# Layer 1's FFN output: sums of weights made by accumulating transfers, and eight pairs in place of seven

## The chip, the core and the metric

One core of a Trainium2 chip runs the whole kernel. The metric is the device time in microseconds, the median of several runs. Engines are called TensorE (PE in the rows, PEld its weight loads), VectorE (DVE), ScalarE (ACT), GpSimd (POOL) and SyncE (SP, which here only issues transfers). A name with a q behind it (SPq) is an engine's instruction queue.

## The reference

Two layers of a streaming encoder on x of 256 tokens by 2048, in float32. The change lies in the last product of the second layer's FFN:

```python
h = rmsnorm(x, norm_ffn[l])
gu = h @ w_ffn_in[l]                                   # 2048 x (2 * 5504)
g = causal_dwconv(gu[..., :D_FF], ffn_conv_w[l], ffn_conv_b[l])
x = x + (jax.nn.silu(g) * gu[..., D_FF:]) @ w_ffn_out[l]   # (256 x 5504) @ (5504 x 2048)
...
return rmsnorm(x, final_norm)
```

Layers are counted from 0: layer 1 is the last.

## The kernel before

**Weights as a stream.** All large weights come from HBM in pieces of 128 partitions by 1024 columns of float32 (512 KB), in the order of their use, into a ring of four buffers `raw`. For each piece ScalarE writes a rounded copy to `whi` (the high half), VectorE writes the rest, `raw - whi`, to `wlo` (the low half), and TensorE takes both. `whi` and `wlo` are rings of four slots too. A float32 product is three matmuls: high by high, high by low and low by high. Each engine walks the pieces in one fixed order, written out by hand; hooks (`at(idx, fn)`) put other work behind a given slot.

**The FFN output.** `hidden` holds the 43 chunks of 128 rows of the hidden layer, as the stationary operand by high and low half. The 2048 output columns are done in two halves u = 0, 1 of 1024, each of which has two strips f of 512 columns (`COLS`) and two blocks t of 128 tokens. A chunk by itself (a "single") has one piece and one slot: four block products, 12 matmuls of 512 columns.

**Pairs by seven products.** Two chunks k1, k2 with two strips and two blocks of tokens are a 2 by 2 block product, which the kernel computes by seven block products in place of eight (Strassen's way, in Winograd's form). This unit takes two pieces, own = (a, b) and second = (d, c), and four slots: "own" (6 matmuls), "fe" (6), "gh" (6) and "d" (3). VectorE makes four sums of the weights: e and f together as one wide addition into the buffer `fe` (line 1188), then g and h into `gh` (lines 1192 and 1194). Their buffers lie in the memory of `gt` and `half`, so the rows show them by these names: `gt<-raw` is the sum fe, `half<-raw,gt` and `half<-raw,half` are g and h, and `wlo<-gt,whi` is the low half of fe. The sums of the hidden layer's blocks ("combinations") are made by VectorE in batches of two pairs (`combs_add`, lines 1203 to 1222, and `combs_low`, 1224), each four or five additions and then a low half, and stay for both halves u.

**The order of units** is given by `units_of`. Both layers have seven pairs, (8, 9), (13, 14) and so on: in half 0 eight singles, then pair, three singles, pair, and so on; in half 1 four singles come first. After the seventh pair half 0 has three and half 1 seven singles. `COMBS_AT` says behind which slot each batch is added; its low half follows one slot later, behind everything that VectorE does for that slot.

**Waits.** ScalarE's high half of slot n waits for TensorE to free slot n - 4 (`slot_released`), VectorE's low half for the high half, TensorE for the low half. SP loads the next piece into a ring buffer when its last reader is through (`wait_read`): for the first piece of a pair this is the sum h, for its second the low half of d. After the last pair of a half the seven products are read out of PSUM: `products_upper` behind the slot five after fe, `products_lower` behind the next; in layer 1 they write to the memory of `gt` and `half` too. TensorE takes the last three slots (`LAST_TAIL`) together: per strip and block, each of the three singles in turn. Then the last strips are added, normalised and stored.

**GpSimd** does a few additions for the mixer of each layer, and nothing in the FFN.

Of the kernel before, what the change touches and what calls it, by code (L numbers as in the profile page):

```python
# [23 lines left out]
LAYERS = 2  # L24
DM = 2048
S = 256
P = 128
# [10 lines left out]
RING = 4  # L38
PB = 8
PIECE = PB * P  # L40
# [17 lines left out]
D0 = CT + 12  # L58
# [9 lines left out]
LO0 = 1  # L68
# [25 lines left out]
COLS = NT * P  # L94
# [13 lines left out]
    return ends  # L108

PAIRED = tuple([(8 + 5 * i, 9 + 5 * i) for i in range(7)] for _ in range(LAYERS))
LEADS = ((8, 4), (8, 4))
PARTS = ("own", "fe", "gh", "d")

def units_of(l, u):

    single = [k for k in range(FC) if not any(k in pair for pair in PAIRED[l])]
    lead, rest = single[:LEADS[l][u]], single[LEADS[l][u]:]
    units = [(k,) for k in lead]  # L120
    for i, pair in enumerate(PAIRED[l]):
        units += [pair] + [(k,) for k in rest[3 * i:3 * i + 3]]
    return units + [(k,) for k in rest[3 * len(PAIRED[l]):]]

def slots_of(l):
# [10 lines left out]
def wraps(piece):  # L137
    return piece % RING == RING - 1

OUT_SLOTS = tuple(slots_of(l) for l in range(LAYERS))
# [5 lines left out]
Q_BANKS = ((4, 5, 6, 7), (0, 1, 2, 3))  # L147
LAST_TAIL = 3
TURN_AT = (1, 1, 3, 3, 5, 5, 6, 6)
COMBS_AT = ((5, 12, 26, 40), (5, 12, 26, 40))  # L150

ENDS = dict(group_ends())
# [24 lines left out]
def program(nc, xT, wstream, params, lamv, consts, poolw, pww, gain_rows, outT):  # L178
# [5 lines left out]
    ALU, ACT, AX = mybir.AluOpType, mybir.ActivationFunctionType, mybir.AxisListType  # L184

    ctx = ExitStack()
    with ctx:
# [8 lines left out]
        def sem(name):  # L196
            return ctx.enter_context(nc.semaphore(name))
# [16 lines left out]
        rest = sb("rest", [P, DM])  # L214
# [6 lines left out]
        raw = sb("raw", [P, RING, PIECE])  # L221
# [135 lines left out]
        front_scaled = [sem(f"front_scaled{t}") for t in range(2)]  # L357
        back_scaled = [sem(f"back_scaled{t}") for t in range(2)]
        sum_ready = sem("sum_ready")
        combs_added, combs_hi, combs_ready = sem("combs_added"), sem("combs_hi"), sem("combs_ready")  # L360
        m1_copied = sem("m1_copied")
        products_read = sem("products_read")
# [28 lines left out]
        def landed(piece):  # L391
            return (piece // RING + 1) * 16
# [13 lines left out]
        def strip(l, u, f, t):  # L406
            c = (2 * u + f) * COLS
            return xt[:, t, c:c + COLS] if l else outs[:, f, t, :]

        block = ctx.enter_context(nc.Block())  # L410

        @block.sync
        def _(sp):
            sp.dma_start(raw[:, 0, 0:PIECE // 2], wstream[0, :, 0:PIECE // 2]).then_inc(half_landed, 16)
            sp.dma_start(raw[:, 0, PIECE // 2:], wstream[0, :, PIECE // 2:]).then_inc(raw_landed[0], 16)

            def load_x(part):
                c, n = X_PARTS[part]
                sp.dma_start(x[:, c:c + n, :], xT[:, c:c + n, :]).then_inc(x_loaded[part], 16)  # L420

            for s in range(1, RING):
                if s > 1:
                    load_x(s)
                sp.dma_start(raw[:, s, :], wstream[s, :, :]).then_inc(raw_landed[s], 16)
            for part in (4, 5):
                load_x(part)

            def load_next(r, s, old):
                sp.wait_ge(lo_ready, old + 1 + LO0)  # L430
                sp.dma_start(raw[:, s, :], wstream[bass.ds(r * RING + s, 1), :, :]
                             .rearrange("o p c -> p (o c)")).then_inc(raw_landed[s], 16)

            def wait_read(l, idx):

                if idx < D0:
                    sp.wait_ge(lo_ready, W0[l] + idx + 1 + LO0)
                    return
                table = OUT_SLOTS[l]
                n = max(m for m, o in enumerate(table) if o[3] <= idx - D0)  # L440
                if table[n][1] != "one" and table[n][3] == idx - D0:
                    sp.wait_ge(sum_ready, SUMS0[l] + 3 * sum(1 for o in table[:n + 1] if o[1] == "d"))
# [30 lines left out]
        def _(act):  # L473
# [28 lines left out]
            for l in range(LAYERS):  # L502
# [179 lines left out]
                def out_hi(n):  # L682

                    u, part, unit, piece = OUT_SLOTS[l][n]
                    s, q = (W0[l] + D0 + n) % RING, sum(1 for o in OUT_SLOTS[l][:n] if o[1] == "d")
                    piece += R0[l] + D0
                    wide = COLS if part == "d" else PIECE
                    if part in ("one", "own"):
                        act.wait_ge(raw_landed[piece % RING], landed(piece))
                        src = raw[:, piece % RING, :]  # L690
                    elif part == "d":
                        act.wait_ge(raw_landed[(piece + 1) % RING], landed(piece + 1))
                        src = raw[:, (piece + 1) % RING, 0:COLS]
                    elif part == "fe":
                        act.wait_ge(sum_ready, SUMS0[l] + 3 * q + 1)
                        src = fe
                    else:
                        act.wait_ge(sum_ready, SUMS0[l] + 3 * q + 3)
# [201 lines left out]
        def _(dve):  # L900
# [30 lines left out]
            for l in range(LAYERS):  # L931
# [236 lines left out]
                def out_lo(n):  # L1168
# [10 lines left out]
                    src = {"one": raw[:, first, :], "own": raw[:, first, :], "fe": fe, "gh": gh, "d": d}[part]  # L1179
                    nc.vector.tensor_tensor(wlo[:, s, 0:wide], src, whi[:, s, 0:wide], ALU.subtract).then_inc(lo_ready, 1)  # L1180
                    if part == "own":
                        dve.wait_ge(raw_landed[second], landed(piece + 1))
                        if q:
                            dve.wait_ge(lo_ready, base + max(m for m in range(n) if OUT_SLOTS[l][m][1] == "gh") + 1 + LO0)
                        if u:
                            dve.wait_ge(products_read, 2 * l + u)
                        a_and_d = raw[:, 0:RING:RING - 1, 0:COLS] if wraps(piece) else raw[:, first:second + 1, 0:COLS]
                        nc.vector.tensor_tensor(fe.rearrange("p (h c) -> p h c", h=2), a_and_d,  # L1188
                                                c[:, None, :].to_broadcast([P, 2, COLS]), ALU.add).then_inc(sum_ready, 1)
                        dve.wait_ge(sum_ready, SUMS0[l] + 3 * q + 1)  # L1190
                        e = fe[:, 0:COLS] if wraps(piece) else fe[:, COLS:PIECE]
                        nc.vector.tensor_tensor(gh[:, 0:COLS], a, e, ALU.add).then_inc(sum_ready, 1)
                        dve.wait_ge(sum_ready, SUMS0[l] + 3 * q + 2)
# [9 lines left out]
                def combs_add(b):  # L1203
# [8 lines left out]
                    pairs = hidden[:, k:k + 5 * n, :].rearrange("p (i j) c -> p i j c", j=5)[:, :, 0:2, :]  # L1212
# [269 lines left out]
        def _(pool):  # L1482
# [6 lines left out]
            for l in range(LAYERS):  # L1489
# [21 lines left out]
                nc.gpsimd.tensor_tensor(win1[:, 1, 15:W], win0[:, 1, 15:W], win0[:, 1, 7:W - 8],  # L1511
                                        ALU.add).then_inc(windowed, 1)
                SEEN["pool"] = st.n

        @block.tensor
        def _(pe):
# [4 lines left out]
            for l in range(LAYERS):  # L1522
# [307 lines left out]
                def seven(n):  # L1830
# [25 lines left out]
                            last.then_inc(acc_done, 1)  # L1856
                        three(C_BANKS[u][0][0], *tokens(k2, 0), *weights(n, 1), False, False).then_inc(slot_free, 1)
                    elif part == "fe":
                        f_at = 1 if wraps(piece) else 0
# [123 lines left out]
```

## Time and profile before

| | us |
|---|---|
| median of 3 runs (2060.15 to 2060.85) | 2060.2 |
| the profiled execution | 2060.9 |
| its span, first to last instruction | 2059.1 |
| busy: TensorE / VectorE / ScalarE / GpSimd | 2046.9 / 1565.3 / 1129.9 / 23.5 |
| layer 1's FFN output, first to last matmul start | 1821.16 to 2051.21 |

The rows are of one profiled execution. Times of a timeline count from the span's start. Busy times of TensorE overlap, since its matmuls are pipelined: the step from one start to the next is what a matmul costs. "Idle before" is the time in which the engine stood still ahead of an instruction, with what ended it behind the arrow.

### The profile page before, as it was taken

Reading aid. Unit: us, or ns where it says so; the run is one execution under the profiler, and the core shown is the slowest. Engines: PE = TensorE matmul, PEld = TensorE weight load, DVE = VectorE, ACT = ScalarE, POOL = GpSimd, SP = SyncE. Lnnn points to the kernel's source line nnn. Section 1 sums busy time; section 2 is a strip of 40 time slices with the busy share of each in tenths; the row PEclk is TensorE's granted clock in tenths of the full one; section 3 lists DMA queues with packets and bytes.
Section 4 is the critical chain, followed back from the end, with each engine's and each line's share of the span. In section 5 each row is a group of like instructions: output and inputs, shape, how many; then the busy total and the mean of one; then the engine's idle time right before and its main releaser. Section 6 shows DMA issues by size and latency. Waiting matters only on the chain.

```text
span 2059.1 us, 31630 instructions
## 1 busy us (share of the span) xinstructions
PE 2046.9 (99%) x11168; PEld 1764.5 (86%) x11168; DVE 1565.3 (76%) x2198; ACT 1129.9 (55%) x1573; POOL 23.5 (1%) x20
## 2 busy tenths in 40 slices
PE   9999999999999999999999999999999999999998
PEld 8888888888888888788888888888888888887887
DVE  7998777676666677988789978677666767679887
ACT  6555655555555555555564556455455555555554
POOL 0001100000000000000000011000000000000000
PEclk9999999999999999999999999999999999999999
DMA  8554355655555655566565544655555565555664
GB/s 292 176 184 164 134 186 182 203 187 194 191 185 182 203 185 183 195 203 199 200 212 196 176 154 144 190 191 191 194 189 188 181 199 190 194 164 194 199 224 170
DMA packets 107942, 389.59 MB, mean 189 GB/s; under 512 B 12112, under 2 KB 12624, under 8 KB 107472
## 3 DMA queue, kind: packets, MB, share of 16 engines
q1 hardware_dynamic: 105984, 383.30, 56.3%
q10 hardware_dynamic: 1872, 5.13, 0.7%
q8 instruction: 56, 0.92, 0.2%
q14 instruction: 30, 0.25, 0.0%
HBM read 386.28 MB, written 2.10 MB: 189 GB/s over the span
## 4 chain that ended last, share of the span: by engine, by line
PE 96%; DVE 3%; ACT 0%; DMA 0%; issue 0%; DVEq 0%; ACTq 0%
PE bank L1524 46%; PE bank L1527 23%; PE bank L1794 6%; PE bank L1796 6%; PE bank L1795 6%; PE bank L1621 2%; PE bank L1600 1%; PE bank L1602 1%; PE bank L1601 1%; DVE wlo L1180 1%; DMA x<-xT 0%; ACT whi L701 0%; PE bank L1674 0%; DVE combs L1227 0%; DVE gt L1188 0%
## 5 line engine op out<-in xcount | busy, mean ns | idle before, releaser
L1524 PE MATMUL bank<-xg,whi 128*128 128x512 f32 x3648 | 1135.8, 393 | 2.1 <-DVE wlo L919 2.1
L938 DVE TENSOR_TENSOR wlo<-raw,whi 128x1024 fp32r<-128x1024 f32 x556 | 676.7, 1223 | 374.2 <-ACT whi L520 373.5
L520 ACT ACTIVATE whi<-raw 128x1024 fp32r<-128x1024 f32 x556 | 582.8, 1057 | 438.8 <-PE bank L1527 419.2
L1527 PEld LDWEIGHTS bank<-xg,wlo 128*128 128x128 f32 x3648 | 685.0, 188 | 151.1
L1527 PE MATMUL bank<-xg,wlo 128*128 128x256 f32 x3648 | 720.0, 279 | 0.0
L1524 PEld LDWEIGHTS bank<-xg,whi 128*128 128x128 f32 x3648 | 552.9, 188 | 6.7 <-issue 3.3
L1180 DVE TENSOR_TENSOR wlo<-raw,whi 128x1024 fp32r<-128x1024 f32 (+1 forms) x164 | 183.1, 1132 | 55.4 <-ACT whi L701 50.6
L1794 PE MATMUL bank<-whi,hidden 128*128 128x512 f32 x548 | 214.4, 391 | 0.9 <-DVE wlo L1180 0.9
L1796 PE MATMUL bank<-whi,hidden 128*128 128x512 f32 x548 | 213.3, 389 | 0.0
L1795 PE MATMUL bank<-wlo,hidden 128*128 128x512 f32 x548 | 213.2, 389 | 0.0
L701 ACT ACTIVATE whi<-raw 128x1024 fp32r<-128x1024 f32 (+1 forms) x164 | 159.4, 984 | 93.3 <-PE bank L1796 82.3
L1524 PE MATMUL bank<-mix,whi 128*128 128x512 f32 x512 | 160.7, 395 | 0.0
L1794 PEld LDWEIGHTS bank<-whi,hidden 128*128 128x128 f32 x548 | 102.9, 188 | 24.0 <-DVE wlo L1180 2.6
L1796 PEld LDWEIGHTS bank<-whi,hidden 128*128 128x128 f32 x548 | 102.9, 188 | 21.5
L1795 PEld LDWEIGHTS bank<-wlo,hidden 128*128 128x128 f32 x548 | 102.9, 188 | 21.0
L525 ACT ACTIVATE half<-bank 128x256 f32<-128x256 f32 x228 | 86.1, 382 | 62.6 <-PE bank L1527 60.1
L1527 PEld LDWEIGHTS bank<-mix,wlo 128*128 128x128 f32 x512 | 96.1, 188 | 21.2
L996 DVE SCALAR_TENSOR_TENSOR gt<-glu,par,gt 128x256 f32<-128x256 f32 x240 | 101.4, 487 | 0.0
L1527 PE MATMUL bank<-mix,wlo 128*128 128x256 f32 x512 | 101.1, 279 | 0.0
L1524 PEld LDWEIGHTS bank<-mix,whi 128*128 128x128 f32 x512 | 78.3, 188 | 0.8
L701 ACT ACTIVATE whi<-gt 128x1024 fp32r<-128x1024 f32 x28 | 29.8, 1063 | 77.3 <-DVE gt L1188 77.3
L1305 DVE SCALAR_TENSOR_TENSOR y<-gt,par,y 128x256 f32<-128x256 f32 x172 | 70.0, 480 | 0.0
(212 smaller groups left out, 1499.2 us busy)
## 6 DMA issues: line engine op xcount, KB each, us to landing
raw<-wstream SPq DMA_DIRECT2D x723, 512.0 KB, 3.4
pw_sb<-pww ACTq DMA_DIRECT2D x2, 1024.0 KB, 7.5
outT<-xt SPq DMA_DIRECT2D x6, 256.0 KB, 2.2
x<-xT SPq DMA_DIRECT2D x2, 512.0 KB, 10.4
gains<-gain_rows ACTq DMA_DIRECT2D x1, 1024.0 KB, 6.0
raw<-wstream SPq DMA_DIRECT2D x2, 256.0 KB, 4.0
x<-xT ACTq DMA_DIRECT2D x2, 256.0 KB, 5.4
x<-xT SPq DMA_DIRECT2D x2, 256.0 KB, 7.6
```

The source lines that it names most:

```text
L520: nc.scalar.activation(whi[:, s, slot_cols(rel)], raw[:, source, :], ACT.Copy).then_inc(hi_ready, 1)
L525: nc.scalar.activation(half[:, i, :], ps[b][:, S:2 * S], ACT.Copy, scale=scales[i]).then_inc(half_ready, 1)
L701: nc.scalar.activation(whi[:, s, 0:wide], src, ACT.Copy).then_inc(hi_ready, 1)
L938: nc.vector.tensor_tensor(wlo[:, s, slot_cols(rel)], raw[:, source, :], whi[:, s, slot_cols(rel)], ALU.subtract).then_inc(lo_ready, 1)
L996: ins = nc.vector.scalar_tensor_tensor(out=gt[:, i, 0:S], in0=glu[:, i, k:k + S], scalar=w, in1=gt[:, i, 0:S], op0=ALU.mult, op1=ALU.add)
L1180: nc.vector.tensor_tensor(wlo[:, s, 0:wide], src, whi[:, s, 0:wide], ALU.subtract).then_inc(lo_ready, 1)
L1305: ins = nc.vector.scalar_tensor_tensor(out=y[:, i, :], in0=gt[:, i, k:k + S], scalar=par[:, bass.ds(col, 1)], in1=y[:, i, :], op0=ALU.mult ...
L1524: nc.tensor.matmul(ps[bank][:], whi[:, s, blk * P:blk * P + P], mov, start=first, stop=False)
L1527: return nc.tensor.matmul(ps[bank][:, 0:S], wlo[:, s, blk * P:blk * P + P], mov[:, 0:S], start=False, stop=last)
L1794: nc.tensor.matmul(ps[bank][:], xh, wh, start=first, stop=False)
L1795: nc.tensor.matmul(ps[bank][:], xh, wl, start=False, stop=False)
L1796: return nc.tensor.matmul(ps[bank][:], xl, wh, start=False, stop=last)
```

## The change

In layer 1 alone, pairs become (8, 9), (12, 13), ... (36, 37): eight of them, at a stride of four. `BETWEEN` gives the singles between two pairs: in half 0 five times two, then two times three; in half 1 four times three, then three times two. After the last pair half 0 has three singles and half 1 has five. The batches of combinations move to slots 5, 13, 25 and 37, and the fourth is full.

In layer 1 the sum fe leaves VectorE. SP loads (a, d) from HBM straight into `fe`, 512 KB in rows of 2 KB, and GpSimd then issues two transfers that add c (256 KB each, from HBM) to its two halves. SP issues the load of the next unit behind the weight load that replaces own, and waits there for the low half of fe; the first waits for the hidden layer to be done, the first of half 1 for the readout of half 0's products. VectorE's g and h, and ScalarE's high half of fe, wait for the second accumulate. VectorE's sums no longer wait for the second piece.

```diff
-PAIRED = tuple([(8 + 5 * i, 9 + 5 * i) for i in range(7)] for _ in range(LAYERS))
+STRIDE = (5, 4)
+PAIRED = tuple([(8 + STRIDE[l] * i, 9 + STRIDE[l] * i) for i in range(n)] for l, n in enumerate((7, 8)))
+BETWEEN = (((3,) * 6, (3,) * 6), ((2, 2, 2, 2, 2, 3, 3), (3, 3, 3, 3, 2, 2, 2)))
+SUMMED = (3, 2)
...
-COMBS_AT = ((5, 12, 26, 40), (5, 12, 26, 40))
+COMBS_AT = ((5, 12, 26, 40), (5, 13, 25, 37))
...
+            owns = own_pieces(1)
+            half_units = len(PAIRED[1])
+            load_fe_behind = {D0 + 4: 0, D0 + owns[half_units - 1] + 6: half_units}
+            for q in range(len(owns) - 1):
+                if q + 1 != half_units:
+                    load_fe_behind[D0 + owns[q]] = q + 1
+
+            def load_fe(q):
+                if q == 0:
+                    sp.wait_ge(hidden_ready, FFG + FFG)
+                elif q == half_units:
+                    sp.wait_ge(products_read, 3)
+                else:
+                    sp.wait_ge(lo_ready, W0[1] + D0 + fe_slots(1)[q - 1] + 1 + LO0)
+                piece = R0[1] + D0 + owns[q]
+                sp.dma_start(fe_halves, wstream[piece:piece + 2, :, 0:COLS].rearrange("o p c -> p o c")).then_inc(fe_landed, 16)
...
                     sp.dma_start(raw[:, piece % RING, :], wstream[piece, :, :]).then_inc(raw_landed[piece % RING], 16)
+                    if l and old - R0[1] in load_fe_behind:
+                        load_fe(load_fe_behind[old - R0[1]])
...
                     elif part == "fe":
-                        act.wait_ge(sum_ready, SUMS0[l] + 3 * q + 1)
+                        if l:
+                            act.wait_ge(fe_summed, 32 * q + 32)
+                        else:
+                            act.wait_ge(sum_ready, SUMS0[l] + SUMMED[l] * q + 1)
...
-                        dve.wait_ge(raw_landed[second], landed(piece + 1))
+                        if l == 0:
+                            dve.wait_ge(raw_landed[second], landed(piece + 1))
...
-                        a_and_d = raw[:, 0:RING:RING - 1, 0:COLS] if wraps(piece) else raw[:, first:second + 1, 0:COLS]
-                        nc.vector.tensor_tensor(fe.rearrange("p (h c) -> p h c", h=2), a_and_d,
-                                                c[:, None, :].to_broadcast([P, 2, COLS]), ALU.add).then_inc(sum_ready, 1)
+                        if l:
+                            dve.wait_ge(fe_summed, 32 * q + 32)
+                            e = fe[:, COLS:PIECE]
...
+            for q, own in enumerate(own_pieces(1)):
+                pool.wait_ge(fe_landed, 16 * q + 16)
+                second = R0[1] + D0 + own + 1
+                for h in range(2):
+                    pool.dma_start(fe_halves[:, h, :], wstream[second, :, COLS:PIECE], accum_op=ALU.add).then_inc(fe_summed, 16)
```

## Rows read from the trace of the kernel before

**Rows 1.** The page: busy time, share of the span, instructions.

```profile
PE 2046.9 (99%) x11168; PEld 1764.5 (86%) x11168; DVE 1565.3 (76%) x2198; ACT 1129.9 (55%) x1573; POOL 23.5 (1%) x20
```

**Rows 2.** Timeline of TensorE in the stage: start, us, engine, line, operation.

```profile
1821.16 0.39 PE L1794 MATMUL bank<-whi,hidden 128*128 128x512 f32 x1
1821.39 0.40 PE L1795 MATMUL bank<-wlo,hidden 128*128 128x512 f32 x1
...
1826.62 1.03 PE L1790 MATMUL bank<-con,x 128*128 128x128 f32 x8
...
2051.21 0.39 PE L1796 MATMUL bank<-whi,hidden 128*128 128x512 f32 x1
```

**Rows 3.** Groups of TensorE from 1821 to 2052 us, first of three lines.

```profile
L1794 PE MATMUL bank<-whi,hidden 128*128 128x512 f32 x274 | 107.3, 392 | 0.5 <-DVE wlo L1180 0.4
...
L1794 PE MATMUL bank<-whi,combs 128*128 128x512 f32 x56 | 22.0, 393 | 0.2
```

**Rows 4.** Waits of TensorE's weight loads, 1820 to 2052: total, times, longest.

```profile
PEld bank L1794 <- DVE wlo L1180: 2.3, 4, 0.6
PEld bank L1794 <- DVE xt L1264: 0.5, 1, 0.5
```

**Rows 5.** Stretches: length, busy PE, PEld, DVE, ACT, POOL, clock, DMA share, GB/s.

```profile
1850.00:1875.00 25.00, 24.69 (x108) 19.79 (x107) 23.69 (x26) 13.15 (x15) 0.00 (x0) 1.00 0.60 204
...
1950.00:1975.00 25.00, 25.00 (x112) 20.72 (x111) 20.14 (x20) 15.68 (x22) 0.00 (x0) 1.00 0.62 207
```

**Rows 6.** Timeline of VectorE around a batch and the sums of the second unit.

```profile
1849.29 1.23 DVE L1180 TENSOR_TENSOR wlo<-raw,whi 128x1024 fp32r<-128x1024 f32 x1 [1.10 <-ACT whi L701]
1850.43 1.22 DVE L1214 TENSOR_TENSOR rest<-hidden 128x1024 f32<-128x1024 f32 x1
...
1853.16 1.22 DVE L1180 TENSOR_TENSOR wlo<-raw,whi 128x1024 fp32r<-128x1024 f32 x1
...
1857.78 1.22 DVE L1188 TENSOR_TENSOR gt<-raw 128x1024 f32<-128x1024 f32 x1
...
1860.37 1.22 DVE L1180 TENSOR_TENSOR wlo<-gt,whi 128x1024 fp32r<-128x1024 f32 x1
```

**Rows 7.** Timeline of TensorE around that batch, and at the last pair.

```profile
1847.93 0.39 PE L1794 MATMUL bank<-whi,combs 128*128 128x512 f32 x1
...
1853.83 0.39 PE L1796 MATMUL bank<-whi,hidden 128*128 128x512 f32 x1
1854.43 0.50 PE L1794 MATMUL bank<-whi,hidden 128*128 128x512 f32 x1 [0.22 <-DVE wlo L1180]
...
1861.16 0.39 PE L1796 MATMUL bank<-whi,hidden 128*128 128x512 f32 x1
1861.64 0.50 PE L1794 MATMUL bank<-whi,combs 128*128 128x512 f32 x1
...
2028.99 0.39 PE L1794 MATMUL bank<-whi,combs 128*128 128x512 f32 x1
```

**Rows 8.** Timeline of VectorE behind the last pair.

```profile
2034.21 0.68 DVE L1241 TENSOR_TENSOR xt<-bank,xt 128x512 f32<-128x512 f32 x1
...
2040.65 3.49 DVE L1180 TENSOR_TENSOR wlo<-raw,whi 128x1024 fp32r<-128x1024 f32 x3
```

**Rows 9.** One weight load issued 1871.7 to 1873, one 1864.4 to 1865.6: KB, us to landing.

```profile
raw<-wstream SPq DMA_DIRECT2D x1, 512.0 KB, 3.2
...
raw<-wstream SPq DMA_DIRECT2D x1, 512.0 KB, 4.4
```

**Rows 10.** Transfers of 256 KB of the whole kernel: count, KB, median us to landing.

```profile
outT<-xt SPq DMA_DIRECT2D x6, 256.0 KB, 2.2
...
poolw_sb<-poolw ACTq DMA_DIRECT2D x2, 256.0 KB, 6.4
```

**Rows 11.** Timeline of GpSimd, layer 1's mixer: two additions of one shape.

```profile
1201.32 2.21 POOL L1494 TENSOR_TENSOR sq<-gt 128x512 f32<-128x512 f32 x1 [962.62 <-DVE gt L996]
...
1217.59 1.29 POOL L1499 TENSOR_TENSOR sq<-y 128x512 f32<-128x512 f32 x1 [12.36 <-ACT y L593]
```

More of the change, by code:

```diff
@@ L121, in units_of @@
     for i, pair in enumerate(PAIRED[l]):
-        units += [pair] + [(k,) for k in rest[3 * i:3 * i + 3]]
-    return units + [(k,) for k in rest[3 * len(PAIRED[l]):]]
+        begin = sum(BETWEEN[l][u][:i])
+        units += [pair] + [(k,) for k in (rest[begin:begin + BETWEEN[l][u][i]] if pair != PAIRED[l][-1] else rest[begin:])]
+    return units
 def slots_of(l):
@@ L359, in program @@
         sum_ready = sem("sum_ready")
+        fe_landed, fe_summed = sem("fe_landed"), sem("fe_summed")
         combs_added, combs_hi, combs_ready = sem("combs_added"), sem("combs_hi"), sem("combs_ready")
@@ L408, in strip, with own_pieces, fe_slots @@
             return xt[:, t, c:c + COLS] if l else outs[:, f, t, :]
+        fe_halves = fe.rearrange("p (h c) -> p h c", h=2)
+        def own_pieces(l):
+            return [o[3] for o in OUT_SLOTS[l] if o[1] == "own"]
+        def fe_slots(l):
+            return [n for n, o in enumerate(OUT_SLOTS[l]) if o[1] == "fe"]
         block = ctx.enter_context(nc.Block())
@@ L441, in wait_read @@
                 if table[n][1] != "one" and table[n][3] == idx - D0:
-                    sp.wait_ge(sum_ready, SUMS0[l] + 3 * sum(1 for o in table[:n + 1] if o[1] == "d"))
+                    sp.wait_ge(sum_ready, SUMS0[l] + SUMMED[l] * sum(1 for o in table[:n + 1] if o[1] == "d"))
                 else:
                     sp.wait_ge(lo_ready, W0[l] + D0 + n + 1 + LO0)
+            owns = own_pieces(1)
[13 more added lines that the diff above has]
+                sp.dma_start(fe_halves, wstream[piece:piece + 2, :, 0:COLS].rearrange("o p c -> p o c")).then_inc(fe_landed, 16)
             def load_each(first, end):
@@ L694, in out_hi @@
                     elif part == "fe":
-                        act.wait_ge(sum_ready, SUMS0[l] + 3 * q + 1)
+                        if l:
+                            act.wait_ge(fe_summed, 32 * q + 32)
+                        else:
+                            act.wait_ge(sum_ready, SUMS0[l] + SUMMED[l] * q + 1)
                         src = fe
                     else:
-                        act.wait_ge(sum_ready, SUMS0[l] + 3 * q + 3)
+                        act.wait_ge(sum_ready, SUMS0[l] + SUMMED[l] * (q + 1))
                         src = gh
@@ L1186, in out_lo @@
                             dve.wait_ge(products_read, 2 * l + u)
-                        a_and_d = raw[:, 0:RING:RING - 1, 0:COLS] if wraps(piece) else raw[:, first:second + 1, 0:COLS]
-                        nc.vector.tensor_tensor(fe.rearrange("p (h c) -> p h c", h=2), a_and_d,
-                                                c[:, None, :].to_broadcast([P, 2, COLS]), ALU.add).then_inc(sum_ready, 1)
-                        dve.wait_ge(sum_ready, SUMS0[l] + 3 * q + 1)
-                        e = fe[:, 0:COLS] if wraps(piece) else fe[:, COLS:PIECE]
+                        if l:
+                            dve.wait_ge(fe_summed, 32 * q + 32)
+                            e = fe[:, COLS:PIECE]
+                        else:
+                            a_and_d = raw[:, 0:RING:RING - 1, 0:COLS] if wraps(piece) else raw[:, first:second + 1, 0:COLS]
+                            nc.vector.tensor_tensor(fe_halves, a_and_d, c[:, None, :].to_broadcast([P, 2, COLS]),
+                                                    ALU.add).then_inc(sum_ready, 1)
+                            dve.wait_ge(sum_ready, SUMS0[l] + SUMMED[l] * q + 1)
+                            e = fe[:, 0:COLS] if wraps(piece) else fe[:, COLS:PIECE]
                         nc.vector.tensor_tensor(gh[:, 0:COLS], a, e, ALU.add).then_inc(sum_ready, 1)
-                        dve.wait_ge(sum_ready, SUMS0[l] + 3 * q + 2)
+                        dve.wait_ge(sum_ready, SUMS0[l] + SUMMED[l] * (q + 1) - 1)
                         nc.vector.tensor_tensor(gh[:, COLS:PIECE], b, gh[:, 0:COLS], ALU.add).then_inc(sum_ready, 1)
@@ L1211, in combs_add @@
                     n = len(PAIRED[l][2 * b:2 * b + 2])
-                    pairs = hidden[:, k:k + 5 * n, :].rearrange("p (i j) c -> p i j c", j=5)[:, :, 0:2, :]
+                    pairs = hidden[:, k:k + STRIDE[l] * n, :].rearrange("p (i j) c -> p i j c", j=STRIDE[l])[:, :, 0:2, :]
                     r = tokens_raw[l][b].rearrange("p (i j c) -> p i j c", i=2, j=2)[:, 0:n]
@@ L1858, in seven @@
                     elif part == "fe":
-                        f_at = 1 if wraps(piece) else 0
+                        f_at = 1 if wraps(piece) and l == 0 else 0
                         last = three(Q_BANKS[u][M5], *comb(0), *weights(n, f_at), first, final)
```

## The prediction

> **What bounds the kernel now.** I read four views in this order: the page's busy times, the waits of TensorE inside the stage that the change touches, the order of VectorE's work just before two of those waits, and the stage by stretches. [rows 1] TensorE is busy for 99% of the span and VectorE for 76%: the end moves only with the number of matmuls or with moments in which TensorE finds no weights. The stage is layer 1's FFN output, from 1821.16 us to the last matmul start at 2051.21 us [rows 2], with (274 + 56) x 3 = 990 matmuls of 512 columns [rows 3]. The mean duration there, 0.39 us, is not the price of one, since they overlap: starts go by in steps of 0.227 us (1821.16, 1821.39; 0.23 as printed) [rows 2]. 990 x 0.2267 = 224.4 us; the four groups of eight transposes take about 1.0 us each [rows 2]; so of the stage's 230.3 us some 1.9 us are stalls. They are few: TensorE's weight loads wait four times for a low half, 2.3 us with what would be idle anyway, and once for a readout [rows 4]. The granted clock is 1.00, the upper of the two levels, throughout [rows 5].
>
> VectorE is close behind. Its busy time is 23.69 of 25 us in a stretch that holds a batch of combinations, 20.14 of 25 us in one without [rows 5]. So the order of VectorE's work decides whether TensorE waits, and less its sum. Its own durations: a full low half 1.22 us, started every 1.14 us; the sum fe 1.22 (1.26 to the next start); the two sums g and h 1.34 together (the low half of fe starts 2.59 us after the sum fe); a batch's additions 2.73 (1850.43 to 1853.16) [rows 6]. What it waits for, in turn, are high halves, and those for TensorE to free one of four slots: the path of the batch at slot 12 starts with TensorE leaving slot 8 at 1847.93 [rows 7] and its low half starts at 1849.29, 1.35 us later [rows 6]. From there VectorE runs without a gap until the low half of fe starts at 1860.37, and TensorE, which was through at 1861.39, starts fe's product at 1861.64 [rows 7]. That is the wait of 0.25 us, and 0.11 us in the next start. I use this way of counting below; it reproduces this case: 1.35 + 1.14 + 2.73 + 1.14 + 1.21 + 2.27 + 1.26 + 1.34 + 1.27 = 13.71 us from slot 8's end against 13.71 us found.
>
> **The matmuls.** A pair by seven products takes 21 matmuls a half, by eight 24. Two units more are 6 matmuls fewer: **-1.36 us**. Transposes, stores and the final normalisation stay. This is all that the change can give on TensorE. Beyond it, only stalls can be saved, 1.8 us at most; so more than 4.1 us (0.2%) faster is nearly out of reach.
>
> **VectorE without the sum fe.** 1.22 us leaves it 14 times (one a unit) [rows 6]; a pair's period falls from 21 + 3 x 12 matmuls (12.9 us) to 21 + 2 x 12 (10.2 us) where two singles lie between. Outside batches VectorE has 1.14 + 1.34 + 2 x 1.14 + 0.61 + 2 x 1.14 = 7.7 us of work in those 10.2 us: no stall. With a batch it is different, and the batches move next to a pair: the additions now follow slot 13, the single directly ahead of own (slot 14), and their low half follows own. From TensorE's leaving the fe slot before: 1.35, low half 1.14, additions 2.73, low half of own 1.14, g and h 1.34, combinations' low half 1.14, low half of fe until TensorE starts 1.27: 10.1 us. TensorE needs for gh, d, two singles and own 39 matmuls: 8.84 us. It waits 1.27 + 0.11 = 1.4 us, at the units i = 1, 3 and 5 of the first half: +4.2 us. Today's two full batches cost 0.60 - 0.23 + 0.11 (1853.83 to 1854.43) and 0.36 each, together 1.7 us [rows 7]: these go. Net **+2.5 us**. The eighth pair also fills up the last batch, which was half as large and made no wait; it is the third of these three.
>
> **The tail.** After the last pair 7 singles follow now, 5 afterwards, while the readout of the second half's products (line 1237 on, eight additions) stays six slots behind. From fe's start D = 2028.99 [rows 7]: the first readout starts at 2034.21 = D + 5.2, the low half between at D + 7.9, and the second ends at 2040.65 = D + 11.7 [rows 8]. Only then comes the low half of slot D's seventh successor, ready for TensorE at D + 12.9. Today the last three slots, which TensorE takes together, begin at D + 14.3, with the seventh behind the readout already in time. Afterwards they begin at D + 3.4 + 2 x 2.72 = D + 8.8, and the third is needed 6 matmuls on, at D + 10.2: TensorE waits 2.7 + 0.1 = **+2.8 us**, right ahead of the end.
>
> **The chain of transfers.** fe becomes a 512 KB load on SP's queue, then two accumulating 256 KB transfers from GpSimd's queue. The load may only go once fe's low half of the unit before is made, since there is one buffer. SP waits for that in line 469's order between two weight loads; the low half comes 1.2 us behind the wait ahead of it and before the one behind it, so no weight load is late by it. The first load waits for the hidden layer, whose last low half follows in the same slot, four slots ahead of its use: hidden. The ninth waits for the third readout, made one slot earlier: hidden too. But in between, a chain closes: low half of fe, C (load and both accumulates), g and h 1.34, low half of fe 1.22, again. It costs C + 2.6 us a unit, C + 3.75 with a batch. VectorE waits with it, with all low halves queued behind, and so does ScalarE with the high half of fe. TensorE gives it 10.2 us, with a batch 11.6 (the 10.2 and the 1.4 above). Over four intervals the stall is 4C + 12.7 - 43.6 = **4 (C - 7.7)**; over five, with the first gap of three singles, 5 (C - 8.2); over six, 6 (C - 8.6); the largest counts. In the second half the four gaps of three (12.9 us) bear C up to 10.3; the three gaps of two cost 3 (C - 7.6) less 2.6 us of lead, as own's low half cannot come more than 5.2 us ahead of fe's product.
>
> What is C? The trace shows no accumulating transfer and none from GpSimd. A 512 KB load lands 3.2 us after its issue when alone, 4.4 about one us behind another [rows 9]. This one goes 1.2 us behind one: 4.4. For the pair of accumulates the nearest rows are 256 KB transfers of the hardware queues: 2.2 us (stores of the result) at best, 6.4 us for the pooling weights [rows 10]. Two in parallel at best 2.5, two in sequence at worst 12.8. I take two of the short ones in sequence, 4.4 us: they share the queues with weight loads that keep the 16 engines busy for about 0.6 of the time [rows 5], and an accumulate also reads its target. C = 8.8, between 5.7 and 18. Then 4 x 1.1 = 4.4 us in the first half and 3 x 1.2 - 2.6 = 1.0 us in the second: **+5.4 us**. The added traffic, 16 MB beside 44, makes single weight loads later; they are issued up to four pieces ahead of their use, three singles or 8.2 us: nothing in the sum, 0 to 2 us in the range.
>
> **Rivals.** (1) *The chain is hidden* (C up to 7.7). For it: a lone load lands in 3.2 us and a store in 2.2. Against it: the load is never alone. Time: 2060.2 + 3.9 = 2064.1, a hair within 0.2%. (2) *VectorE is not late either*, the one that ends on the other side: the place is the low half of fe at the units with a batch. If TensorE's lead there is 1.3 us more than I count, and the tail's lead 2.7 us more, the chain being hidden as well, what remains is -1.4 and up to -1.7 of today's stalls: 2057.1 to 2060, say 2058. For it: VectorE loses 14 x 1.22 us of work. Against it: the same counting gives today's stall exactly. (3) *GpSimd's work stretches beside VectorE's.* The same addition of 128x512 on GpSimd takes 2.2 us in one place and 1.3 us in another, and VectorE may be what differs [rows 11]. If the making of each of two transfers is stretched by 0.9 us, C is 10.6: 12.0 us in the first half by the six-interval form, and in the second 3 x 3.0 - 2.6 = 6.4 and 4 x 0.3 = 1.2: 2060.2 + 3.9 + 19.6 = 2083.7. With C = 12, from accumulates at the slow end of the rows, 6 x 3.4 = 20.4 and 4 x 1.7 + 3 x 4.4 - 2.6 = 17.4 us: 2102. (4) *The change does less than it says*, if the second accumulate starts only at the first one's end; this is C again, and within its bounds.
>
> The Trainium skill, "SBUF — State Buffer", section "Who interferes with whom", states that a VectorE operation with two SBUF inputs holds off a GpSimd instruction which reads SBUF, and its rules for kernel authors advise against hiding a GpSimd-queue DMA under VectorE work; all that VectorE does in this stage has two inputs. By that rule rival 3 would hold; the same section infers that making descriptors needs the write side only, which would spare it. The rows on GpSimd's additions agree with the rule, not yet for transfers.
>
> **Chances.** Forecast (C 7.8 to 10.3, 2064.5 to 2079): 0.42. Rival 1: 0.26. Rival 2: 0.11. Rival 3, with slower accumulates (rival 4 among them): 0.18, two thirds of it for C near 10.6. Something faster than 2056.1: 0.03. A measurement of this kernel can tell about 0.2%, 4.1 us, from no change. Slower by more: 0.42 + 0.18 and a little of rival 1, 0.61; within: 0.36; faster: 0.03. The range runs from rival 2's 2059 to C = 11: 2060.2 + 3.9 + 6 x 2.4 + (4 x 0.7 + 3 x 3.4 - 2.6) = 2089. The forecast's own is 2064.5 to 2079.
>
> **What would show it.** The page: 6 matmuls fewer at the two lines of the FFN output, no sum fe on VectorE in layer 1. Combinations: a gap of about 1.3 us in TensorE's starts ahead of fe at the second, fourth and sixth unit. Tail: a gap of 2.7 us, 6 matmuls into the last 36. Chain: VectorE's first g addition waits for the accumulates, and ScalarE's high half of fe too; from unit to unit the distance is C + 2.6 where it is over 10.2 us. Issue to landing of the accumulates gives C outright. The prediction is wrong if these waits end well before TensorE's lead is used up, or if weight loads become what is waited for.

## The result

| | us |
|---|---|
| before, median of 4 | 2060.5 |
| changed kernel, median of 4 (2134.2 to 2138.3) | 2135.7 |
| ratio, 95% interval | 1.0366 (1.0353 to 1.038) |
| changed kernel's profiled span; before | 2134.5; 2059.1 |

The change costs 75 us. Slower was forecast, at 2069.5; the time lies far above the range's end of 2089.

The first view is who waited for whom in the stage, for the changed kernel (engine, line, what it waited for: us in total, times, longest). Lines have moved: 1232 is the sum g (1192 before), 1215 the low half (1180), 736 the high half (701), 1840 to 1842 the three matmuls.

```profile
ACT whi L736 <- DMA gt<-wstream: 86.8, 15, 8.7
DVE half L1232 <- DMA gt<-wstream: 76.5, 16, 7.0
PEld bank L1840 <- DVE wlo L1215: 56.4, 15, 4.9
...
PE bank L1840 <- DVE wlo L1215: 50.1, 15, 4.5
...
ACT whi L736 <- DMA raw<-wstream: 12.2, 5, 4.2
```

In [rows 4] four waits for a low half came to 2.3 us; here 15 come to 56.4, and the engine ahead of them, VectorE, waited 16 times for `gt<-wstream`, the transfers into fe. That is every unit. ScalarE found a weight piece missing five times, but each of the 16 waits for the sum g ended with an accumulate, and VectorE stood idle for 1.2 us or more before it: no late piece held a unit up. The chain of the second unit's low half of fe to the third's, as the trace links it (start, us, what):

```profile
1859.83 1.14 DVE wlo L1215
1860.97 0.02 issue
1860.99 4.40 DMA gt<-wstream
1865.39 0.28 issue
1865.67 0.54 POOL gt L1559
1866.21 7.12 DMA gt<-wstream
...
1873.42 0.70 DVE half L1232
...
1874.15 0.69 DVE half L1234
1874.84 1.14 DVE wlo L1215
```

This is the loop of the prediction: low half of fe, load, accumulates, g, h, low half of fe. C is 1873.42 - 1860.99 = 12.4 us here, not 8.8. The load with its way to GpSimd takes 4.7 of it (4.4 forecast), the pair of accumulates 7.75 (4.4 forecast), from GpSimd's first issue to the sum g. Over the 15 units behind the first, from the load's issue to the sum g, C is 11.5 to 14.9 us, 13.4 in the mean, of which the pair takes 6.7 to 10.2, 8.5 in the mean.

What the transfers take, by issue in the stage (count, KB, median us to landing), as against [rows 9, 10]:

```profile
raw<-wstream SPq DMA_DIRECT2D x75, 512.0 KB, 5.1
gt<-wstream POOLq DMA_DIRECT2D x31, 256.0 KB, 7.1
gt<-wstream SPq DMA_DIRECT2D x15, 512.0 KB, 4.5
```

TensorE at the third unit: it stops at 1871.12 and finds the low half of fe at 1876.03.

```profile
1870.89 0.39 PE L1841 MATMUL bank<-wlo,hidden 128*128 128x512 f32 x1
1871.12 0.39 PE L1842 MATMUL bank<-whi,hidden 128*128 128x512 f32 x1
1876.03 0.50 PE L1840 MATMUL bank<-whi,combs 128*128 128x512 f32 x1 [4.52 <-DVE wlo L1215]
1876.36 0.56 PE L1841 MATMUL bank<-wlo,combs 128*128 128x512 f32 x1
1876.73 0.63 PE L1842 MATMUL bank<-whi,combs 128*128 128x512 f32 x1
```

The steps behind the gap widen from 0.23 to 0.37 and then to 0.43 us: the granted clock falls to the lower of its two levels (0.50 from 1876.5 to 1879.5 us) for some nine matmuls and comes back. A stretch of the changed kernel, beside [rows 5] (the 0.80 is the mean granted clock):

```profile
2050.00:2075.00 25.00, 18.82 (x63) 14.54 (x62) 14.67 (x16) 10.34 (x11) 1.76 (x2) 0.80 0.68 193
```

### The profile page after: what moved, and what is told of

Its sections match the earlier page's. It is cut to its first block, busy times and chain, and to the rows that moved or that the text cites. A ratio compares the mean times of both kernels' runs of the same rounds, so it can differ in the third digit from the quotient of the medians.

```text
span 2134.5 us, 31670 instructions
## 1 busy us (share of the span) xinstructions
PE 2072.4 (97%) x11162; PEld 1779.4 (83%) x11162; DVE 1556.0 (73%) x2192; ACT 1131.8 (53%) x1577; POOL 51.8 (2%) x52
## 3 DMA queue, kind: packets, MB, share of 16 engines
q0 software_dynamic: 4608, 8.39, 2.4%
## 4 chain that ended last, share of the span: by engine, by line
PE 84%; DMA 10%; DVE 4%; issue 1%; POOL 0%; ACT 0%; DVEq 0%; ACTq 0%; SPq 0%
PE bank L1570 45%; PE bank L1573 23%; DMA gt<-wstream 9%; PE bank L1840 3%; PE bank L1842 3%; PE bank L1841 3%; PE bank L1667 2%; DVE wlo L1215 2%; PE bank L1646 1%; PE bank L1648 1%; PE bank L1647 1%; DVE half L1232 1%; DVE half L1234 1%; POOL gt L1559 0%; DMA x<-xT 0%
## 5 line engine op out<-in xcount | busy, mean ns | idle before, releaser
L1840 PE MATMUL bank<-whi,combs 128*128 128x512 f32 x120 | 55.9, 466 | 48.0 <-DVE wlo L1215 47.8
## 6 DMA issues: line engine op xcount, KB each, us to landing
x<-xT SPq DMA_DIRECT2D x2, 512.0 KB, 10.3
```

The lines of the kernel that those rows point to most:

```text
L1840: nc.tensor.matmul(ps[bank][:], xh, wh, start=first, stop=False)
```

## The experiments

The theory: one buffer for fe closes a loop from unit to unit, and its time C, mis-sized, is the whole miss. The rivals: the traffic (16 MB more, the engines' share of time up from 0.6) makes weights late; VectorE's new order; the stretching of GpSimd's work. Each time below is the median of its runs, with the kernel before at 2060.4 to 2060.5 beside it.

**The chain opened.** A second buffer, and loads that go two units ahead:

```diff
+            fe2 = sb("fe2", [P, PIECE], f32, no_windows)
...
-                    load_fe_behind[D0 + owns[q]] = q + 1
...
+                    load_fe_behind[D0 + owns[q - 2]] = (q,)
...
-                    sp.wait_ge(lo_ready, W0[1] + D0 + fe_slots(1)[q - 1] + 1 + LO0)
+                    sp.wait_ge(lo_ready, W0[1] + D0 + fe_slots(1)[q - (1 if q == half_units else 2)] + 1 + LO0)
```

> The changed kernel with a second buffer for fe, in memory that the mixer no longer needs, so that a load waits for fe's low half of the unit before the last. All transfers stay. Theory (the chain over one buffer): it is open now, since load and accumulates (12.4 us measured) have two units (20.4 us) in place of one; what remains is the six matmuls less, VectorE's order at the batches and the tail, 3.9 us together: 2064 us, between 2061 and 2068, and VectorE waits for no accumulate. Rival (the traffic of 16 MB more makes weight loads late, or descriptors and VectorE hold each other up): the transfers are all still there, so most of the 75 us stay, over 2100 us.

2068.8 us, ratio 1.0042 (1.0028 to 1.0057). 67 of the 75 us are gone with every transfer still made. VectorE waits for an accumulate only once, at the first unit:

```profile
ACT whi L751 <- DMA gt<-wstream: 5.5, 1, 5.5
DVE half L1247 <- DMA gt<-wstream: 4.2, 1, 4.2
```

**Loads without accumulates**, on one buffer:

```diff
-                            dve.wait_ge(fe_summed, 32 * q + 32)
+                            dve.wait_ge(fe_landed, 16 * q + 16)
...
-                for h in range(2):
-                    pool.dma_start(fe_halves[:, h, :], wstream[second, :, COLS:PIECE], accum_op=ALU.add).then_inc(fe_summed, 16)
```

> The changed kernel without the two accumulating transfers: fe is the loaded (a, d) alone, so c is left out of the sums; VectorE and ScalarE wait for the load. One buffer. Theory (chain): C falls from 12.4 to the load's 4.6 us and the chain is hidden (it bears 7.7): 2064 us, and a gap of about 1.3 us ahead of fe at the units 1, 3 and 5 and of 2.5 us in the last 36 matmuls. Rival (VectorE's new order is the larger part): well over 2070 us. Rival (traffic): half of the added bytes remain, 2080 to 2100 us.

2065.8 us, ratio 1.0025 (1.0016 to 1.0035). Here the two terms of the sum that are VectorE's stand alone. TensorE ahead of fe at the second unit, and in the last 36 matmuls (steps of 0.23 without a gap):

```profile
1858.64 0.50 PE L1837 MATMUL bank<-whi,combs 128*128 128x512 f32 x1 [1.10 <-DVE wlo L1215]
...
2047.60 0.50 PE L1837 MATMUL bank<-whi,hidden 128*128 128x512 f32 x1 [2.56 <-DVE wlo L1215]
```

The starts before these are at 1857.15 and 2044.65. So the waits are 1.49 - 0.23 = 1.26 us and 2.95 - 0.23 = 2.72 us; 1.27 and 2.7 were forecast. The other two batches give 1.48 us each between starts. Its span is 2062.2, 3.1 us over before, where 3.9 was forecast. The median of its ten executions is 5.4 over: three lie at 2064.0 to 2064.2, seven at 2065.7 to 2066.4. The profiled one is of the three, and its clock did not fall behind the gap in the tail. That it fell there in the seven is likely (early_first below shows it, with 1.5 us lost), but their traces are not kept.

**The order alone**, with the sum fe on VectorE and no transfers:

```diff
-SUMMED = (3, 2)
+SUMMED = (3, 3)
...
-                            dve.wait_ge(fe_summed, 32 * q + 32)
-                            e = fe[:, COLS:PIECE]
...
+                            nc.vector.tensor_tensor(fe_halves, a_and_d, c[:, None, :].to_broadcast([P, 2, COLS]),
+                                                    ALU.add).then_inc(sum_ready, 1)
```

> Eight pairs in the new order, but the sum fe made by VectorE as before, no added transfers. Theory: the sum's 1.26 us lies on VectorE's path at the units with a batch: 3 x (1.27 + 1.26 + 0.11) = 7.9 us, less 1.7 of today's stalls, less 1.4 of matmuls, plus 2.8 for the tail: +7.6, 2068 us. Rival (order is what costs 75 us): 2130 us or more. Rival (VectorE is not late): under 2062 us.

2071.8 us, ratio 1.0053 (1.0036 to 1.007): the order is not what costs 75 us. The three gaps are 2.74, 2.74 and 2.73 us between starts, 2.51 us of wait against 2.53 counted. The profiled execution, at 2072.6 us, is 4.6 over the forecast 2068, and the clock is as much: behind two of these three gaps and behind the tail's, the next seven or eight steps add up to 1.5 to 1.6 us more than at the full clock (most are 0.42 or 0.43 us in place of 0.23).

**The transfers alone**, in the old order of seven pairs, one buffer:

```diff
-STRIDE = (5, 4)
+STRIDE = (5, 5)
...
-BETWEEN = (((3,) * 6, (3,) * 6), ((2, 2, 2, 2, 2, 3, 3), (3, 3, 3, 3, 2, 2, 2)))
+BETWEEN = (((3,) * 6, (3,) * 6), ((3,) * 6, (3,) * 6))
...
-COMBS_AT = ((5, 12, 26, 40), (5, 13, 25, 37))
+COMBS_AT = ((5, 12, 26, 40), (5, 12, 26, 40))
```

> The old order with seven pairs and three singles between, with the transfers in place of VectorE's sum fe in layer 1, one buffer. Theory (chain): a unit takes C + 2.6 (with a batch 3.8), 15 to 16.5 us as in the changed kernel, against 12.9 us of matmuls: 12 gaps with 2.5 to 3.5 us, less a lead of 5 us, and slower matmuls after each gap: 2090 to 2110 us. Rival (the stride and the order of batches are what costs): 2060 us, no change.

2109.4 us, ratio 1.0239 (1.0222 to 1.0256). The loop costs 49 us where three singles lie between, too. Its C over the 12 gaps inside the halves is 14.4 us in the mean, and 12 x (14.4 - 10.3) gives 49.

**What C is made of.** First the pair of transfers as plain copies from the same queue:

```diff
-                    pool.dma_start(fe_halves[:, h, :], wstream[second, :, COLS:PIECE], accum_op=ALU.add).then_inc(fe_summed, 16)
+                    pool.dma_start(fe_halves[:, h, :], wstream[second, :, COLS:PIECE]).then_inc(fe_summed, 16)
```

> The changed kernel with the two transfers from GpSimd's queue as plain copies in place of accumulating ones: they overwrite fe, so the sums are not made. One buffer, same bytes from HBM. It splits C = 12.4 us (load 4.6, then 7.8 for the pair). Theory A (the accumulate itself is slow, as it reads its target and adds): the pair falls to 3.5 to 4.5 us, C to 8.5, 2064 to 2072 us. Theory B (GpSimd's queue is slow, the making of transfers or their completion): the pair stays near 7 to 8 us, 2115 to 2136 us.

2103.6 us, ratio 1.0203 (1.0188 to 1.0219): between the two theories. The same chain as above, in this kernel:

```profile
1859.09 4.65 DMA gt<-wstream
1863.74 0.28 issue
1864.02 0.53 POOL gt L1559
1864.55 5.04 DMA gt<-wstream
...
1869.68 0.70 DVE half L1232
```

The pair takes 5.7 us from GpSimd's first issue (1864.02) to the sum, 7.75 with accumulation; over the units in which VectorE waited for it, 6.4 and 8.5 in the mean. In the median a transfer lands 5.1 us after its issue as a copy and 7.1 as an accumulate. So 2 us are the accumulation's, and the plain copy of 256 KB from this queue, 5.1 us beside weight loads, is 2.9 us dearer than the store of [rows 10]; in this kernel a load of 512 KB into fe from SP's queue lands in 4.4. An accumulate also holds the transfer engines twice as long for the same bytes. GpSimd's queue from 1821 to 2127 us, in the changed kernel and then in this one (packets, MB, share of the 16 engines' time):

```profile
q0 software_dynamic: 4608, 8.39, 16.7%
...
q0 software_dynamic: 2560, 8.39, 7.9%
```

The second issue goes 0.5 us behind the first as a copy and about 0.9 us as an accumulate (the two span 1.07 and 1.76 us).

Then one accumulate of 512 KB in place of two:

```diff
-                for h in range(2):
-                    pool.dma_start(fe_halves[:, h, :], wstream[second, :, COLS:PIECE], accum_op=ALU.add).then_inc(fe_summed, 16)
+                pool.dma_start(fe_halves, wstream[second, :, None, COLS:PIECE].to_broadcast([P, 2, COLS]),
+                               accum_op=ALU.add).then_inc(fe_summed, 16)
```

> The changed kernel with one accumulating transfer of 512 KB, whose source names c twice, in place of two of 256 KB. One buffer. If a fixed part of each transfer counts (an issue takes 0.9 to 1.1 us of GpSimd, one behind the other), C falls by 1 to 2 us and 15 units gain it: 2105 to 2120 us. If the amount of data decides (theory A), C stays within 0.5 us: 2128 to 2140 us. If a long transfer is worse, over 2140 us.

2136.2 us, ratio 1.0361 (1.0345 to 1.0377): no change against two. It lands 8.2 us after its issue, as late as the second of the pair (0.9 + 7.1). It was forecast that a second fixed part on the path would show as a gain of 1 to 2 us a unit; C is 13.6 us in the mean here against 13.4, so the number of transfers is not what costs.

**Early first load.** Two buffers, the first unit's load six slots earlier (into the buffer that needs no wait for the hidden layer), the second's one slot later. The edit is against two_buffers:

```diff
-            load_fe_behind = {D0 + 4: (0, 1), D0 + owns[half_units - 1]: (half_units,),
-                              D0 + owns[half_units - 1] + 6: (half_units + 1,)}
+            load_fe_behind = {D0 - 2: (0,), D0 + 5: (1,), D0 + owns[half_units - 1] + 6: (half_units + 1,)}
...
```

> Two buffers as in two_buffers, but the first unit's load goes six slots earlier, into the second buffer, and the second unit's one slot later. In two_buffers both went together, fe's first sum came 4.2 us late, ScalarE was held by it and TensorE waited 1.9 us for a transposed copy, with slower matmuls behind (3.6 us in all). Theory: this goes, and the time is that of the run with loads alone, 2065 us (2063 to 2067). Rival (two_buffers lost its 3 us to traffic spread over the stage): 2068 to 2069 us.

2065.9 us, ratio 1.0026 (1.0016 to 1.0035): the time of the kernel with loads alone (2065.8), with all accumulates made. With the chain open, the accumulates and their traffic cost nothing that these runs can tell. The added loads are in both kernels, and the 3.1 us of load_only against 3.9 counted without any traffic leave no room for theirs. This is so though the share of the transfer engines' time over 1840 to 2040 us is 0.89 (length, busy PE, PEld, DVE, ACT, POOL, clock, share, GB/s):

```profile
1840.00:2040.00 200.00, 196.64 (x867) 161.39 (x867) 159.10 (x170) 111.66 (x124) 24.55 (x28) 1.00 0.89 273
```

In the kernel before the same stretch has 0.60, in load_only 0.73. Two_buffers' 3 us came from ScalarE: held by the first fe until 1842.85, it copied a transposed bank late.

**A version that is faster.** Early_first with VectorE's order mended at both places that the counting names:

```diff
-BETWEEN = (((3,) * 6, (3,) * 6), ((2, 2, 2, 2, 2, 3, 3), (3, 3, 3, 3, 2, 2, 2)))
+BETWEEN = (((3,) * 6, (3,) * 6), ((2, 2, 2, 2, 2, 3, 3), (3, 3, 2, 2, 2, 2, 2)))
...
-COMBS_AT = ((5, 12, 26, 40), (5, 13, 25, 37))
+COMBS_AT = ((5, 12, 26, 40), (5, 18, 30, 42))
...
-                    at(D0 + n, combs_add, b)
+                    if l and b:
+                        at(D0 + n - 4, combs_add, b, 0)
+                        at(D0 + n, combs_add, b, 1)
...
```

> As early_first, with two more edits. A batch's additions are split: the wide one behind own of the second unit of each couple, the four small ones behind the first single after it, the low half behind the second. The tail after the last pair gets its seven singles back: half 1 has (3, 3, 2, 2, 2, 2, 2) between. Counting as in the prediction: fe is ready 1.3 us ahead of TensorE at the batches, the first single 0.7, the next fe 0.05; no gap at batches, none in the tail. -1.4 for the matmuls and -1.7 for today's two batches: 2060.4 - 3.0 = 2057.4 us, between 2056.5 and 2060; faster than the kernel before by 0.1 to 0.2%. Rival (VectorE's work has no more room): gaps elsewhere, 2060 to 2065 us.

2058.6 us, ratio 0.999 (0.9981 to 0.9999), about 2 us faster than before (0.2 to 3.9 by the interval), 1 us above the expectation. No gap at the second and fourth unit and none in the tail. At the sixth one is left, and it traces back to a weight load: ScalarE waited 1.51 us for a weight piece, own came late, and with it fe, 0.54 us between starts beyond the usual step:

```profile
1893.10 1.06 ACT L752 ACTIVATE whi<-raw 128x1024 fp32r<-128x1024 f32 x1 [1.51 <-DMA raw<-wstream]
...
1899.07 0.50 PE L1863 MATMUL bank<-whi,combs 128*128 128x512 f32 x1 [0.38 <-DVE wlo L1231]
```

**What the transfers bring once the chain is open.** First the old order of seven pairs with early_first's two buffers and loads; as seven is odd, the first load of half 1 here takes the buffer of the unit before it and waits for that unit's low half:

```diff
-STRIDE = (5, 4)
+STRIDE = (5, 5)
...
-BETWEEN = (((3,) * 6, (3,) * 6), ((2, 2, 2, 2, 2, 3, 3), (3, 3, 3, 3, 2, 2, 2)))
+BETWEEN = (((3,) * 6, (3,) * 6), ((3,) * 6, (3,) * 6))
...
-COMBS_AT = ((5, 12, 26, 40), (5, 13, 25, 37))
+COMBS_AT = ((5, 12, 26, 40), (5, 12, 26, 40))
```

> The old order with seven pairs, the sum fe by transfers as in early_first (two buffers). It shows what the transfers cost or bring by themselves once the chain is open; with one buffer this order took 2109 us. Theory: VectorE has 1.26 us less ahead of each fe, so the second of today's two waits at each full batch goes (0.36 us each), the first stays: 2060.4 - 0.7 = 2059.7 us, between 2058.5 and 2061. Rival (the traffic, at 0.8 to 0.9 of the engines' time, makes weight pieces late often): 2062 to 2066 us.

2060.4 us, ratio 0.9999 (0.999 to 1.0008). The expected 0.7 us is below what the runs can tell; in the trace the second wait at each full batch (0.48 between starts before) is gone, and the first, 0.60, is there.

Then the order of spread on order_alone, where the sum fe is VectorE's and nothing is loaded:

```diff
-BETWEEN = (((3,) * 6, (3,) * 6), ((2, 2, 2, 2, 2, 3, 3), (3, 3, 3, 3, 2, 2, 2)))
+BETWEEN = (((3,) * 6, (3,) * 6), ((2, 2, 2, 2, 2, 3, 3), (3, 3, 2, 2, 2, 2, 2)))
...
-COMBS_AT = ((5, 12, 26, 40), (5, 13, 25, 37))
+COMBS_AT = ((5, 12, 26, 40), (5, 18, 30, 42))
...
+                        at(D0 + n - 4, combs_add, b, 0)
...
```

> The order, the split batches and the tail of spread, with the sum fe made by VectorE and no added transfers. Theory: two units with a batch hold 2 x 8.96 + 3.9 = 21.8 us of VectorE's work against 20.4 us of matmuls: 1.4 us short three times, less at most 2.6 us of lead, with clock losses behind longer gaps: 2060 to 2064 us; the transfers of spread bring 2 to 5 us. Rival (the transfers bring nothing, the gain of spread is its order): 2057 to 2059 us, as spread.

2061.1 us, ratio 1.0002 (0.9993 to 1.0011): two gaps of 1.44 and 1.45 us at batches. Its profiled span is 2058.7, that of spread 2056.4. So with the chain open the transfers earn 2.5 us in the new order (all 11 times of spread, 2057.4 to 2060.0, lie below all 11 of this kernel, 2060.2 to 2061.4), and in the old one nothing that the runs can tell.

## Why the prediction was wrong

- **Matmuls, -1.4 us.** Six fewer, as said. No run isolates it.
- **VectorE at the batches, +2.5 us.** Right in size and place: 1.25 or 1.26 us of wait against 1.27, three times each in load_only, two_buffers and early_first, where the chain doesn't cover it, and 2.51 against 2.53 with the sum left on VectorE.
- **The tail, +2.8 us.** Right: 2.72 us of wait against 2.7. In the changed kernel it is 2118.19 - 2115.51 - 0.23 = 2.45 us.
- **The chain's form.** Right. With the measured C, C + 2.6 us a unit and 1.15 more at the three batches gives 14 x 16.18 + 3.45 = 230.0 us for the 14 gaps between units that don't span the two halves (C 13.58 in their mean). The sums g start at 1841.54 and 2100.06, and the gap between the halves is 28.93: 258.52 - 28.93 = 229.6 us.
- **The size of C: the step that failed.** The step was "I take two of the short ones in sequence, 4.4 us": it priced accumulates from GpSimd's queue by the store of a hardware queue, the cheap end of its own bounds of 5.7 to 18 us. The pair took 8.5 us in the mean (7.75 at the third unit), 6.4 of which a pair of plain copies from this queue takes as well, and 2 the accumulation. The load was near: 4.4 forecast, 4.5 in the median, 4.9 with its way to GpSimd in the mean. As the stall grows by 6 us in the first half and up to 7 in the second for each us of C, 4.6 us too little (13.4 against 8.8) is most of the miss. By the prediction's forms, with each half's own C over these gaps: 6 x (13.33 - 8.6) = 28.4 and, since C is over 10.3 and no lead is left to take off, 4 x 3.55 + 3 x 6.25 = 33.0 at C = 13.85. Together that is 61 us where 5.4 stood. TensorE's own starts agree: from fe of the second unit to fe of the eighth 97.7 us pass (1861.01 to 1958.72) where 294 matmuls need 66.7, and 2.8 of the rest are counted at the batches; from the ninth to the last it is 115.0 (1987.65 to 2102.66), where 363 need 82.3. The bounds were there; the range took them in up to C = 11 alone. (By the same forms the forecast's own upper end, C = 10.3, is 2080 and not 2079.)
- **"The ninth waits for the third readout, made one slot earlier: hidden too."** Wrong: a step that was not worked out. The load goes behind a low half that comes only after both parts of the readout, 5.3 us of VectorE, at 1973.53 against a sum g of 1956.11 for the unit before; it lands with its accumulates at 1985.0. From unit to unit 28.9 us passed, where the matmuls need 3.4 + 7 x 2.72 + 1.36 = 23.8: 5 us. And 2.6 us of lead, which I took off in the second half, did not exist with gaps of three chain-bound as well; it is left out of the 33.0 above.
- **The clock was not in the sum.** In the chain's stretch next to nothing is to be seen of it, as TensorE waits anyhow and the distances come out of C alone. In the tail it does: from fe of the last unit (2102.66) to the last start (2126.52) pass 23.9 us, where 75 matmuls at 0.227 take 16.8; the wait is 2.45, and the starts that are 0.4 us apart are most of the remaining 4.6.
- **Rivals.** "The chain is hidden" and "VectorE is not late either" are refuted. The traffic as a cost of its own, 0 to 2 us in the range, was right with the chain open: at most 0.5 to 0.7 us in one run's trace. Rival 3's direction was right, its mechanism is not what the traces show. GpSimd is taken for 1.75 us by the issue of two accumulates, whether VectorE is idle all the while or busy all the while (length, busy PE, PEld, DVE, ACT, POOL, clock, share, GB/s; first seven_pairs, then spread):

```profile
1899.62:1901.37 1.75, 1.75 (x9) 1.48 (x8) 0.00 (x0) 0.46 (x1) 1.75 (x2) 1.00 1.05 368
...
1861.78:1863.53 1.75, 1.75 (x9) 1.46 (x8) 1.75 (x2) 1.75 (x3) 1.75 (x2) 1.00 1.06 377
```

- **VectorE's work and the pair.** In the changed kernel the pair issued at 1865.67 took 7.75 us with VectorE busy for 0.77 us of them, the one at 1848.88 8.39 us with 6.25, and the longest, at 2008.54, 10.20 us with 2.54. So VectorE's work does not set the pair's time, and the rule by which rival 3 would hold (the Trainium skill, "SBUF — State Buffer", "Who interferes with whom") is not borne out for the issue of transfers; the inference of the same section, which spares it, fits.
- **Weight loads and the pair.** What does go with the pair's time is the number of weight loads issued in the 4.5 us behind GpSimd's first issue: with none it took 7.1 us in the mean (3 units of the changed kernel), with one 8.65 (7 units), with two 9.1 (5 units). In one_accumulate it is 7.5, 8.5 and 10.2. The prediction let the added traffic delay weight loads alone; here loads and accumulates seem to delay each other inside the loop. No run changes the weight loads by themselves, so how much of the pair's 8.5 us is theirs stays open.
- **The estimate for two transfers.** The one by the Trainium skill, "DMA: Bandwidth & Descriptors", 3.2 us for two, is not borne out: plain copies took 5.7 here, beside weight loads, and the measurement decides.

In sum: 61 us of chain by the formula, 5 at the change of halves, 3.9 as forecast and some 4.6 of clock in the tail make 75 us; 75.4 lie between the two spans.

## What to carry to other kernels

A transfer that refills a buffer inside a loop adds its full latency to the loop, issue to landing and all hops, not its bandwidth. Write the loop's time down as a sum. If an unknown in it is multiplied by the number of turns, its upper bound belongs into the forecast, or a second buffer into the kernel: it took away 67 of 75 us here with every transfer kept. A price read from a transfer on another queue, in another direction and with less traffic beside it is a guess, as the 2.2 us of a store was for 7.1. Counting from "TensorE frees the slot" through the waiting engine's own order reproduces waits to 0.02 us, and shows where the work should go instead.

## What the runs showed of the hardware

- From GpSimd's queue a 256 KB copy from HBM to SBUF landed 5.1 us after its issue, an accumulate 7.1, and one accumulate of 512 KB 8.2, beside weight loads; a 512 KB load from SP's queue took 4.5.
- For the same 8.39 MB, accumulates took 16.7% of the transfer engines' time over 306 us and plain copies 7.9%.
- The issue of two accumulates kept GpSimd for 1.75 us with VectorE idle (seven_pairs, 1899.62) and with VectorE busy throughout (spread, 1861.78).
- At a share of 0.89 of the transfer engines' time, 273 GB/s (early_first and spread), only one of TensorE's waits traced back to a late weight piece; at 0.60 none did. The landing of a weight load rose from 3.4 us to between 5.1 and 5.6.
- In order_alone, load_only, two_buffers and early_first TensorE waited seven times for 2.50 to 2.73 us. Behind four of these waits the granted clock fell to the lower level (0.50) for seven or eight matmuls, most of them in steps of 0.43 in place of 0.227 us, 1.5 to 1.6 us in all; behind three it did not. It fell too behind two_buffers' wait of 2.0 us ahead of a transpose. Behind the nine waits of some 1.25 us in the last three of these kernels it never did. Behind the same gap of 2.95 us in the tail it fell in early_first and not in load_only, 2063.8 against 2062.2 us of span.
